# Scan products placed at later steps, low key parts on the vector engine, and a table addition in four pieces

## The reference

```python
# layer 0: one input projection, then two branches side by side
q, kc, vc, ks, vs, kw, vw, gl, u = split(rms_norm(x) @ w_in)
#  NSA, 8 heads in 2 groups: compressed + selected + window attention, gated
#    compress(rows): hid = chunks[n] @ w1[0] + chunks[n+1] @ w1[1] + pos @ w1
#                    kc, vc = gelu(hid) @ w2        (kc then RMS-normed)
#  S5, 32 channel groups x 64 complex states, fed by u
bu = einsum('gpc,btgc->btgp', b, ug);  x = w * bu
s  = associative_scan(a * s_prev + x)              # over time
y  = einsum('gcp,btgp->btgc', c, s) + d * u
out = z * sigmoid(z @ w_glu + b_glu),  z = gelu(y)
x = x + concat(nsa, out) @ w_out;  x = x + conv_ffn(rms_norm(x))
# layer 1: sliding-window attention (128 keys), 16 heads, sinks, position bias table
s = q @ k.T * 64**-0.5 + bias;  p = softmax(s with sink);  o = p @ v
x = x + o @ w_out;  x = x + conv_ffn(rms_norm(x))
```

## Time and profile before

| | us |
|---|---|
| median of 3 timed runs (3144.67 to 3147.86) | 3145.43 |
| the profiled execution's own time | 3140.55 |
| its span | 3138.8 |
| PE busy | 2935.9 (94%) |
| DVE, ACT, POOL busy | 1432.6, 946.2, 768.8 |
| mean granted PE clock | 0.951 of full |

### The profile page before, as it was taken

The page is one execution under the profiler, slowest core; times in us unless marked ns, Lnnn a source line. Parts: engine busy times, 40 slices in busy tenths (PEclk is TensorE's granted clock), DMA queues, the critical chain, the costliest instruction groups (busy, mean ns, idle before and its releaser), DMA issues. The chain is left out here.

```text
span 3138.8 us, 51059 instructions
## 1 busy us (share of the span) xinstructions
PE 2935.9 (94%) x19701; PEld 2817.5 (90%) x19701; DVE 1432.6 (46%) x3225; ACT 946.2 (30%) x1697; POOL 768.8 (24%) x552
## 2 busy tenths in 40 slices
PE   7997987789998699999999999989799999999998
PEld 6997886589996599999999999968799999999998
DVE  4517783467775424432432443157734432442441
ACT  4223444355553232111211123057632211111111
POOL 1123552042112132222222123142132222222221
PEclk9998998869999799999999999979999999999999
DMA  6323453131003311111111111110111111111112
GB/s 174 86 83 112 143 160 86 35 115 42 2 1 156 143 49 36 51 47 47 40 49 47 45 49 46 36 56 2 28 44 41 47 47 45 49 43 45 53 43 74
DMA packets 270117, 195.93 MB, mean 62 GB/s; under 512 B 56388, under 2 KB 260286, under 8 KB 263407
## 3 DMA queue, kind: packets, MB, share of 16 engines
q1 hardware_dynamic: 262859, 143.19, 15.9%
q0 software_dynamic: 6912, 50.33, 4.4%
q10 hardware_dynamic: 184, 0.20, 0.0%
HBM read 176.64 MB, written 24.42 MB: 64 GB/s over the span
## 5 line engine op out<-in xcount | busy, mean ns | idle before, releaser
L590 PE MATMUL ps<-xf_hi,w_hi 128*128 128x344 f32 x2352 | 756.7, 322 | 9.9 <-POOL w_lo L581 9.9
L592 PE MATMUL ps<-xf_hi,w_lo 128*128 128x344 f32 x2352 | 753.2, 320 | 0.0
L591 PE MATMUL ps<-xf_lo,w_hi 128*128 128x344 f32 x2352 | 752.4, 320 | 0.0
L581 POOL TENSOR_TENSOR w_lo<-w_raw,w_hi 128x1024 fp32r<-128x1024 f32 (+1 forms) x162 | 384.9, 2376 | 1448.5 <-ACT w_hi L577 1448.5
L590 PEld LDWEIGHTS ps<-xf_hi,w_hi 128*128 128x128 f32 x2352 | 443.6, 189 | 11.3 <-issue 11.2
L591 PEld LDWEIGHTS ps<-xf_lo,w_hi 128*128 128x128 f32 x2352 | 443.4, 189 | 0.7 <-issue 0.7
L592 PEld LDWEIGHTS ps<-xf_hi,w_lo 128*128 128x128 f32 x2352 | 443.4, 189 | 0.0
L590 PE MATMUL ps<-hid_hi,w_hi 128*128 128x344 f32 x1056 | 339.4, 321 | 0.0
L592 PE MATMUL ps<-hid_hi,w_lo 128*128 128x344 f32 x1056 | 337.6, 320 | 0.0
L591 PE MATMUL ps<-hid_lo,w_hi 128*128 128x344 f32 x1056 | 336.9, 319 | 0.0
L577 ACT CAST w_hi<-w_raw 128x1024 fp32r<-128x1024 f32 (+1 forms) x162 | 165.6, 1022 | 388.9 <-PE ps L592 384.0
(11 more groups left out here) (570 smaller groups left out, 5367.6 us busy)
## 6 DMA issues: line engine op xcount, KB each, us to landing
w_raw<-in_ffn_w_up_dram SPq DMA_DIRECT2D x44, 512.0 KB, 3.7
w_raw<-in_ffn_w_gate_dram SPq DMA_DIRECT2D x44, 512.0 KB, 3.7
w_raw<-in_ffn_w_down_dram SPq DMA_DIRECT2D x32, 448.0 KB, 3.6
w_raw<-in_ffn_w_down_dram SPq DMA_DIRECT2D x16, 512.0 KB, 3.7
w_raw<-in_a_w_in_dram SPq DMA_DIRECT2D x14, 512.0 KB, 4.1
w_raw<-in_c_w_in_dram SPq DMA_DIRECT2D x10, 512.0 KB, 3.9
residual<-hT SPq DMA_DIRECT2D x1, 4128.0 KB, 13.3
hT<-residual SPq DMA_DIRECT2D x1, 4128.0 KB, 17.6
```

The costliest lines, as they stand in the source:

```text
L581: pool.tensor_tensor(self.parts.lo[:, slot, 0:kt, :], self.raw[:, slot, 0:kt, :], self.parts.hi[:, slot, 0:kt, :].bitcast(F32), ALU.subtra ...
L590: pe.matmul(psum, w_hi, x_hi, start=(a == 0), stop=False)
L591: pe.matmul(psum, w_hi, x_lo, start=False, stop=False)
L592: ins = pe.matmul(psum, w_lo, x_hi, start=False, stop=(a == kt - 1))
```

## The change

Three parts.

1. In the first layer's `stage_before_attend` the eight low parts leave POOL for DVE, in five places of its list; and DVE's copy of `baseT` (L2846) goes ahead of `near_bias(0)` and `hidden(0)`.
2. In `SwaStart` the table addition becomes four operations of four heads each, and the last chunk's low parts go to the end of DVE's list.
3. The scan's tasks get a table of their own for quarter 0 (Q0 at step 13 instead of 1, KM at 15 instead of 3, Y0 at 28 instead of 18, SEC_EVEN at 31 instead of 25), and are 6, 3 and 0 steps later in quarters 1 to 3 (at most step 31). Where X or XS tasks then stand behind step 17, `hidden(2q)` runs in front of them.

```diff
+                if rows:
+                    rows.vector_last(dve)
...
-        near = a.btab[:, :, 0:P]
-        pool.tensor_tensor(near, near, bc(far, [[0, CHD], [1, P]]), ALU.add).then_inc(self.s_table, 1)
-        pool.wait_ge(self.s_table, 1)
+        for h in range(0, CHD, 4):
+            near = a.btab[:, h:h + 4, 0:P]
+            pool.tensor_tensor(near, near, bc(far, [[0, 4], [1, P]]), ALU.add).then_inc(self.s_table, 1)
+        pool.wait_ge(self.s_table, CHD // 4)
...
-        self.keys_low(pool, 2)
...
+    def vector_last(self, dve):
+        cols, src, dst = self.key_cols(2), self.kvT[:, 0, :], self.keys
+        dve.wait_ge(self.s_khi, 12)
+        for g in range(G):
+            rows = slice(g * HD, (g + 1) * HD)
+            for half in range(2):
+                dve.tensor_tensor(dst.lo[half * HD:(half + 1) * HD, g, cols], src[rows, cols],
+                                  dst.hi[rows, g, cols].bitcast(F32), ALU.subtract)
...
+AT_FIRST = dict(Q0=13, Q1=14, KM=15, Q2=16, Q3=17, SEC_ODD=18, X0=20, X1=21, X2=22, XS0=23, XS1=24, Y0=28, Y1=29, YS=30,
+                SEC_EVEN=31)
+LATER = [0, 6, 3, 0]
+def step_of(name, q):
+    if q == 0:
+        return AT_FIRST[name]
+    return min(AT[name] + LATER[q], STEPS - 1)
...
-                        if m == AT["SEC_EVEN"] - 1:
+                        if m == step_of("SEC_EVEN", q) - 1:
                             gelu(2 * q)
...
                     for x in range(3):
...
+                        if not summed and step_of(name, q) > 17:
+                            hidden(2 * q)
+                            summed = True
                         dve.wait_ge(s_ps, where[name, q] + 1)
...
-                    hidden(2 * q)
+                    if not summed:
+                        hidden(2 * q)
...
-            low(0)
             pool.wait_ge(s_qk, 1)
...
-            low(1)
...
+            for g in range(G):
+                for half in range(2):
+                    low(0, g, half)
 
             dve.wait_ge(s_qk, 1)
             dve.tensor_reduce(small[:, 0:1], k.ps[0:64, 4, 0:NCS], AX, ALU.max, negate=True).then_inc(s_max, 1)
+            low(1, 0, 0)
...
+            dve.wait_ge(s_t, 1)
+            dve.tensor_copy(m.bT[0:16, :], k.ps[0:16, 6, 128:192]).then_inc(s_tc, 1)
             near_bias(0)
             hidden(0)
-            dve.wait_ge(s_t, 1)
-            dve.tensor_copy(m.bT[0:16, :], k.ps[0:16, 6, 128:192]).then_inc(s_tc, 1)
...
+            low(1, 0, 1)
+            low(1, 1, 0)
             dve.wait_ge(s_root, 1)
...
+            low(1, 1, 1)
```

More of the change, by code:

```diff
@@ L2019, with at_step @@
 STEPS = 32
-def at_step(n):
-    return [name for name, step in AT.items() if step == n]
+AT_FIRST = dict(Q0=13, Q1=14, KM=15, Q2=16, Q3=17, SEC_ODD=18, X0=20, X1=21, X2=22, XS0=23, XS1=24, Y0=28, Y1=29, YS=30,
[5 more added lines that the diff above has]
+    return min(AT[name] + LATER[q], STEPS - 1)
+def at_step(n, q):
+    return [name for name in AT if step_of(name, q) == n]
 def stage_s5_compress(k, s, uT, cin, posb, kc, vc):
@@ L2230, in _ @@
                             products(n - 1)
-                        for name in at_step(m):
+                        for name in at_step(m, q):
                             if (name, q) in where:
@@ L2297, in _ @@
                             by_step(q)
-                        if m == AT["SEC_EVEN"] - 1:
+                        if m == step_of("SEC_EVEN", q) - 1:
                             gelu(2 * q)
-                        if q and m == AT["SEC_ODD"] - 1:
+                        if q and m == step_of("SEC_ODD", q) - 1:
                             gelu(2 * q - 1)
-                        for name in at_step(m):
+                        for name in at_step(m, q):
                             if (name, q) in where:
@@ L2385, in _ @@
                     link(dve.tensor_tensor(hn, hn, tmp, ALU.add))
+                    summed = False
                     for x in range(3):
@@ L2776, in _, with low @@
             ins.then_inc(s_qb, 1)
+            def low(x, g, half):
+                dst, src = pairs[x]
+                rows = slice(g * HD, (g + 1) * HD)
+                dve.wait_ge(s_khi, 4 * x + 2 * g + 2)
+                dve.tensor_tensor(dst.lo[half * HD:(half + 1) * HD, g, :], src[rows, :], dst.hi[rows, g, :].bitcast(F32),
+                                  ALU.subtract)
             dve.wait_ge(s_gtr, 1)
```

## The result

| us | before | after |
|---|---|---|
| median of five timed runs each | 3145.4 | 3129.6 |
| lowest and highest | 3139.9, 3147.9 | 3125.4, 3132.8 |
| profiled execution: own time, span | 3140.6, 3138.8 | 3129.6, 3127.8 |
| mean granted PE clock | 0.951 | 0.956 |
| PE busy, POOL busy | 2935.9, 768.8 | 2930.9, 744.7 |

The ratio of after to before is 0.9956, 95% interval 0.9943 to 0.9968: 14 us faster, 10 to 18. A second set of nine runs gave 0.9966 (0.9952 to 0.998), 11 us. So the direction and the rough size came out. The parts did not, and the reader should look at those. Of the signs that the prediction names, the first attention's start moved by 0.7 us (668.49 to 667.84) and not by 6 to 7.

The account below looks back on a forecast made before the run. PE, busy for 94% of the span, was taken as the bound, so only its idle or half-clock stretches could give time. Scan 4.0, before the first attention 2.7, second layer 1.8: 8.5 us, 3145.4 to 3136.9; range 3130 to 3143.5.

Parts of the forecast that it names:

- V was ready at 251.1: Scan, quarter 0: DVE's first table V is ready before step 13 asks at about 252, so PE's 15.8 us wait goes.
- The step behind it: Scan, quarter 0: from KM's copy to PE's release by the `Tg` DMAs pass 27.95 us, so Y0 starts at 285.7.
- The next one: Scan, quarter 0: YS's copy to `s_fin` takes 15.7 us, less up to 2; `s_fin` at 314, `by_step` ends at 316.
- `hidden(2q)` ahead of X0 or XS0 costs nothing: Scan, DVE's list: after quarter 0's Pm2 DVE idles until X0, and the four additions fit there, at no cost.
- rival A: Scan: the loop eats the gain, each quarter handing on its delay; last `by_step` not before 461; 3140.9 us; chance 0.21.
- The `baseT` copy: Before the first attention: the copy ahead of the bias work cuts PE's 2.38 us wait for `baseT`, bringing 1.9 us.
- the low parts: Before the first attention: moving the first layer's eight low parts from POOL to DVE brings 0.8 us.
- Rival E: Before the first attention: low parts on DVE don't shorten the stage, ACT and PE carrying its chain; 3139.6 us; chance 0.07.
- Rival C: First attention: the shorter `baseT` wait keeps PE's clock up, some 16 us more gained; 3121 us; chance 0.05.
- Its price per microsecond: First attention: each microsecond of PE at half clock costs 0.36 us, from 79 instructions in 16 us against 124.
- Rival D: First attention: the moved instructions prolong half clock; gain gone from 24 us on, 3153 us at 45; chance 0.04.
- a scan term of 4.0: Scan stage, all quarters: 4.0 us gained through the later tasks, with ends of -4 and +10.

Follow-up runs that it names:

- The version with the sums ahead: After with hidden(2q) ahead of turns(q+1) in quarters 2 and 3, and the first GELU at step 25 instead of 30; ratios to before 0.9937 and 0.994.

## Why the forecast came out as it did

**The scan, first quarter: the failed step is "V was ready at 251.1".** I took DVE's time from an execution in which POOL idled beside it. Once PE no longer waits, POOL's copies run and DVE's table V is complete 4.5 us later than before (255.37 for 250.91); PE reached V's place and waited 4.05. KM's copy ended at 262.9 for 257.8 and Y0 came at 291.78 for 285.7. The step behind it held: 28.8 us from that copy to the release by `Tg`, for 27.95. The next one was mis-sized the other way. From YS's copy to `by_step` I had 15.7 us and up to 2 less, and it took 11.3. The second miss takes back somewhat over half of the first: `by_step` at 317.0 for 314. The new wait for `chunksT` is there, as the prediction put it.

**Quarters 1 to 3: the failed step is "`hidden(2q)` ahead of X0 or XS0 costs nothing", with the waits for the GELU left out of the sum.** In quarter 2 `hidden(4)` does not stand there: XS0 is at step 15, so it stays behind `turns(3)`, and PE waits 3.3 us for its GELU and then runs at half clock for some 6 us. The second `by_step` came 1.6 us better than forecast (388.6 for 390.2), the third 5.7 worse (463.7 for 458). Moving those four additions gave a stage of 304.4 and 304.5 us, which is 6 below the old table's mean. So the order of tasks that the change chose can bring what I had forecast for it and more, but not with this list on DVE. Waits for the GELU were in the profile of before, 2.8 us in all.

**What the scan's part brought** is 0.4 us between means, with the old table's executions spread over 9 us: rival A in outcome, and the last `by_step` passed A's mark of 461. Its mechanism (each quarter hands on its delay) is not what the profile shows: the second `by_step` was earlier by more than the first (3.5 and 2.3 us), and quarter 2 lost that with its GELU. By timing, the scan's part alone is at 0.9991, and after at 0.9956 where the kernel without that part is at 0.9958: neither tells it from nothing.

**Before the first attention** both terms were mis-sized. The `baseT` copy was to bring 1.9 and brought 0.3 (42.2 for 42.5), the low parts 0.8 and brought 5.6 in their own run, 4.0 in the mean. I had compared one DVE row with its neighbour and taken the excess of that pair for the whole; five more rows of the same stage were held up, and the wait for `baseT` was itself one of the results. Rival E is refuted. A rule of the Trainium skill (GPSIMD Engine Reference, 8. Key points) names the operations: besides DVE instructions with two SBUF inputs also those in a 2-port mode. The prediction had weighed it with the first half alone, though its own row of 2.24 us has one tensor as input, and counted it against the change. The trace agrees with the first half (2.73 and 3.27 us for 0.68 and 1.22). The cast and the TENSOR_SCALAR rows, with one tensor as input, were held up as well (1.71, 1.51, 2.31), as the second half would have it, but in which mode they ran no trace here shows. The reduction beside them was not held up (0.68 and 0.68).

**The second layer** gave 2.1 us where 1.8 were forecast in the executions with half clock in its first sums, and the end moved to ACT and DVE as said; the table in pieces, which I put at 0, is worth about 2 more in the others.

**The clock.** Rival C gave the ledger's largest row, 6.3 us, but as a draw of this one pair: the first attention was long in 2 of 14 executions, and whether the low parts make that rarer stays open. Its price per microsecond held: half clock ended 20.0 us sooner behind the attention's first product, times 0.36 is 7.2, for 6.3 measured. Rival D did not come. The new wait of 9.5 us in quarter 1 did put PE at half clock, as the prediction said: the granted clock was 0.5 from 315 to 324 us.

So that the total was near is luck: a scan term of 4.0 brought nothing that can be told from 0, the two other terms brought 4.0 + 2.7 = 6.7 in the means for my 4.5, and a shorter first attention, forecast at 0, adds 2.3 of which it is open whether the change earned it. The version with the sums ahead is at 0.9937 and 0.994, against after's 0.9956 and 0.9966.

## What to carry to other kernels

When an elementwise operation moves from GpSimd to VectorE, price not only its own duration but every VectorE row that ran beside it, against the same row in a place where GpSimd idles; and when a wait of PE goes, expect GpSimd to wake up beside VectorE. A wait that stands behind a wait is worth what is left when both are out of the way, so try the second one alone. And profile the unchanged kernel several times before a stage's difference of a few microseconds is called an effect: here one stage of one program took 307 to 316 us.

## What the runs showed of the hardware

- A VectorE instruction of the kinds above stands until GpSimd's current instruction ends, however small it is: 64x16 took 1.51 us for 0.17, 18x344 3.56 us, each ending within 0.4 us of GpSimd's end. Cutting a GpSimd instruction in four cost it 0.7 us (4.51 to 5.22) and cut that wait. Where it started and GpSimd's next instruction came 0.01 us behind it, VectorE's ran at its usual 0.68 us, and GpSimd's took 2.88 us for 2.34.
- One program's scan stage (the old table) took 307.1, 308.2, 310.6, 310.6, 311.1, 314.4, 315.9 and 307.1 us. The three longest have 6.9 to 8.5 us of waits for the GELU and the three shortest 2.8 to 3.1, but one of 310.6 has 2.8 too. Behind such a wait in quarter 1 or 2 the granted clock was 0.5 for some 6 us. In these quarters the rows of `turns` on VectorE tell the two cases apart: 15.7 to 16.1 us in all in the six quarters with such a wait, 14.3 to 14.8 in the ten without. Why they are longer in some is open. The new table took 309.8, 309.9 and 311.0, with the same waits each time.
- The half clock at the start of the first attention ended 29 to 31 us behind the attention's first product in twelve executions and 49 and 53 us behind it in two, with PE busy for 48.5 of the 49 us and 52.5 of the 53.
